# Attention values as 64-column weights, a transposed attention gate and probabilities scaled before their transpose, in a hybrid decoder layer

## What is computed

```python
u = rms_norm(h, norm_gain[layer])
z = jnp.einsum('bsd,de->bse', u, w_in[layer])
...
y_a = dsa_attention(q_a, k_a, v_a, q_i, k_i, w_i, topk).reshape(B, S, ATT_WIDTH)
y_a = y_a * jax.nn.silu(g_a)
...
y_r = retention(q_r, k_r, v_r).reshape(B, S, RET_V_WIDTH)
y_r = y_r * jax.nn.silu(g_r)
mix = jnp.concatenate([y_a, y_r], axis=-1)
h = h + jnp.einsum('bse,ed->bsd', mix, w_out[layer])
```

## Time and profile before

| | |
|---|---|
| median of 3 runs (lowest to highest) | 289.85 us (289.65 to 290.09) |
| the profiled execution, its own time | 289.56 us |
| its span in the profile | 287.8 us |
| PE busy | 280.0 us, 97% |
| DVE busy | 201.7 us, 70% |
| ACT busy | 143.1 us, 50% |
| POOL busy | 66.1 us, 23% |
| granted TensorE clock, mean | 0.994 |

### The profile page before, as it was taken

One profiled execution on the slowest core, in us unless ns is written; L12 is line 12 of the kernel. 1 busy time (PEld: TensorE's weight loads), 2 busy tenths in 40 slices (PEclk: granted clock), 3 DMA queues, 4 the chain that ended last, 5 costly groups with the idle time before them and its releaser, 6 DMA issues.

```text
span 287.8 us, 4402 instructions
## 1 busy us (share of the span) xinstructions
PE 280.0 (97%) x1506; PEld 239.7 (83%) x1506; DVE 201.7 (70%) x416; ACT 143.1 (50%) x305; POOL 66.1 (23%) x121
## 2 busy tenths in 40 slices
PE   8999999999999999999999999999999999999992
PEld 7998788888888788888888788888888888888891
DVE  3875879999999999999947545658734733763342
ACT  5887656526455224584357452583444563351230
POOL 1028822222200078766400102021020020000211
PEclk9999999999999999999999999999999999999997
DMA  7998404220422043052212220302200407311113
GB/s 268 410 365 336 147 3 146 73 68 8 146 74 75 20 146 110 18 146 75 75 48 98 75 73 0 122 26 74 76 0 2 146 0 260 107 36 36 75 78 142
DMA packets 13989, 30.10 MB, mean 105 GB/s; under 512 B 1168, under 2 KB 1680, under 8 KB 13968
## 3 DMA queue, kind: packets, MB, share of 16 engines
q1 hardware_dynamic: 13392, 29.04, 30.4%
q10 hardware_dynamic: 576, 0.79, 0.7%
HBM read 27.73 MB, written 2.10 MB: 104 GB/s over the span
## 4 chain that ended last, share of the span: by engine, by line
PE 65%; DVE 20%; issue 3%; POOL 1%; ACT 1%; POOLq 0%; DVEq 0%
PE bank L447 16%; PE bank L449 15%; PE bank L448 15%; PE bank L498 6%; DVE keys L1095 6%; DVE top L1093 5%; DVE w_lo L994 3%; PE bank L512 3%; DVE keys L1080 2%; PE bank L528 2%; PE bank L527 2%; DVE k_stack L1056 2%; PE bank L537 1%; PE bank L559 1%; PE bank L572 1%
## 5 line engine op out<-in xcount | busy, mean ns | idle before, releaser
L447 PE MATMUL bank<-w_hi,xT_hi 128*128 128x512 f32 (+1 forms) x296 | 116.5, 394 | 0.5 <-DVE w_lo L994 0.5
L449 PE MATMUL bank<-w_hi,xT_lo 128*128 128x512 f32 (+1 forms) x296 | 114.0, 385 | 0.0
L448 PE MATMUL bank<-w_lo,xT_hi 128*128 128x512 f32 (+1 forms) x296 | 113.8, 385 | 0.0
L447 PEld LDWEIGHTS bank<-w_hi,xT_hi 128*128 128x128 f32 x296 | 55.7, 188 | 11.6 <-DVE w_lo L994 1.2
L449 PEld LDWEIGHTS bank<-w_hi,xT_lo 128*128 128x128 f32 x296 | 55.6, 188 | 11.5
L448 PEld LDWEIGHTS bank<-w_lo,xT_hi 128*128 128x128 f32 x296 | 55.8, 188 | 9.8
L994 DVE TENSOR_TENSOR w_lo<-w_raw,w_hi 128x1024 fp32r<-128x1024 f32 x36 | 45.1, 1273 | 13.9 <-ACT w_hi L629 13.6
L629 ACT ACTIVATE w_hi<-w_raw 128x1024 fp32r<-128x1024 f32 x36 | 37.5, 1055 | 5.2 <-PE bank L449 3.4
L749 ACT ACTIVATE work<-work,small 128x128 f32<-128x128 f32 (+3 forms) x32 | 17.7, 555 | 31.8 <-DVE small L1118 31.7
L1093 DVE MAX8 top<-keys 128x8 f32<-128x256 f32 (+2 forms) x48 | 26.9, 560 | 1.3
L932 POOL TENSOR_TENSOR th<-zt,tab 128x64 f32<-128x64 f32 (+1 forms) x24 | 12.6, 523 | 60.0 <-ACT zt L678 56.4
(11 more groups left out here) (130 smaller groups left out, 370.9 us busy)
## 6 DMA issues: line engine op xcount, KB each, us to landing
w_raw<-in_w_in SPq DMA_DIRECT2D x28, 512.0 KB, 4.2
w_raw<-in_w_out SPq DMA_DIRECT2D x8, 512.0 KB, 3.7
retT<-in_x SPq DMA_DIRECT2D x8, 256.0 KB, 3.8
x_h<-in_first SPq DMA_DIRECT2D x2, 836.0 KB, 8.1
out<-x_h SPq DMA_DIRECT2D x4, 320.0 KB, 2.5
mix<-in_first SPq DMA_DIRECT2D x3, 418.0 KB, 5.2
v_ret<-in_x SPq DMA_DIRECT2D x2, 512.0 KB, 11.5
v_att<-in_x SPq DMA_DIRECT2D x2, 512.0 KB, 5.8
```

Source lines behind the costliest of these rows:

```text
L447: pe.matmul(o, xh, hi[:, kk, c0:c0 + w], start=first, stop=False)
L448: pe.matmul(o, xh, lo[:, kk, c0:c0 + w], start=False, stop=False)
L449: mm = pe.matmul(o, xl, hi[:, kk, c0:c0 + w], start=False, stop=last)
```

## The change

- `values(s)`: the weights are now the 64 columns of v of one head and the probabilities (128 columns) move; the two heads of a pair write PSUM partitions 0 to 63 and 64 to 127. So the attention output comes out transposed (`attT`) and only the retention half of `mix` is transposed (`transpose_mix`, four transposes instead of eight).
- The softmax divisor can no longer be applied to rows afterwards: `reciprocal(s)` (DVE) and `scale_probs(s)` (ACT) divide the probabilities before their transpose, which waits for `p_scaled` instead of `exp_done`.
- The attention gate's group is computed transposed (weights `w_hi`, moving `xT_hi` and `xT_lo`, again 24 matmuls of 512 columns). Its RMS factor then varies along the columns: POOL spreads it, PE transposes it (`turn_rstd`, slot 15), ACT writes `half_rstd_row`.
- The attention gate comes in slots 24 to 27 and the retention gate in 28 to 31. Outputs of blocks 0 and 1 wait in `qT` (`stash_y`).
- In a batch the scores come first. On ACT `probT_out` and `ret_squares` stand behind `exps`; on DVE `masked_max` stands ahead of the gates and of `decayed`, and `reciprocal` behind one top-k round. The rounds are 3 a slot up to slot 15 (before 17), 2 after.

```diff
@@ CHUNKS and constants
+          ("att_gate", 3 * ATT_W, ATT_W),
+          ("ret_gate", BASE + IDX_W + 2 * RH * RQK + RH * RV, RH * RV)]
...
-        n = min(4 if g <= 9 else 3 if g <= 17 else 2, ROUNDS * (MT - 1) - done)
+        n = min(4 if g <= 9 else 3 if g <= 15 else 2, ROUNDS * (MT - 1) - done)
@@ tensor
                     if g >= GROUPS:
-                        pe.wait_ge(mixlo_done, 2 * (m + 1))
+                        pe.wait_ge(att_lo_done, m + 1)
+                        pe.wait_ge(ret_lo_done, m + 1)
...
+                    if c == C_AG:
+                        e = slice(m * P, (m + 1) * P)
+                        pe.matmul(o, hi[:, kk, e], xT_hi[:, k, :], start=first, stop=False)
+                        pe.matmul(o, lo[:, kk, e], xT_hi[:, k, :], start=False, stop=False)
+                        mm = pe.matmul(o, hi[:, kk, e], xT_lo[:, k, :], start=False, stop=last)
+                        continue
...
             def values(s):
...
-                if p == 0 and b >= 1:
-                    pe.wait_ge(y_att_psum, b)
-                for hh in range(2):
-                    h = 2 * p + hh
-                    pe.wait_ge(pt_evac, 2 * s + hh + 1)
-                    for j in range(b + 1):
-                        mm = pe.matmul(att_ps[:, h * HD:(h + 1) * HD], probT[:, hh, j * P:(j + 1) * P],
-                                       v_att[:, j, h * HD:(h + 1) * HD], start=(j == 0), stop=(j == b))
+                if p == 0 and 1 <= b <= STASHED:
+                    pe.wait_ge(y_stashed, b)
+                elif p == 0 and b > STASHED:
+                    pe.wait_ge(att_mixed, b)
+                pe.wait_ge(pt_evac, 2 * s + 2)
+                for j in range(b + 1):
+                    for hh in range(2):
+                        h = 2 * p + hh
+                        mm = pe.matmul(att_ps[64 * hh:64 * hh + 64, p * P:(p + 1) * P], v_att[:, j, h * HD:(h + 1) * HD],
+                                       probT[:, hh, j * P:(j + 1) * P], start=(j == 0), stop=(j == b))
...
             def transpose_probs(s):
...
-                    pe.wait_ge(exp_done, 2 * s + hh + 1)
+                    pe.wait_ge(p_scaled, 2 * s + hh + 1)
...
-                        if s == steps_before_mix(m):
-                            pe.wait_ge(mixlo_done, 2 * m + hh + 1)
+                        if hh and s == steps_before_mix(m):
+                            pe.wait_ge(ret_lo_done, m + 1)
...
             def transpose_mix(m):
-                pe.wait_ge(att_mixed, m + 1)
                 pe.wait_ge(ret_mixed, m + 1)
                 pe.wait_ge(pt_evac, 2 * steps_before_mix(m))
...
+                if m >= 1:
+                    pe.wait_ge(ret_lo_done, m)
+                for j in range(KH):
+                    e = ATT_W + j * P
+                    mm = pe.transpose(trans_ps[1][:, j * P:(j + 1) * P], mix[:, m, e:e + P], ident)
+                mm.then_inc(mixT_mm, 1)
@@ scalar
+            def scale_probs(s):
+                b = s // PAIRS
+                act.wait_ge(rden_done, s + 1)
+                for hh in range(2):
+                    pr = prob[:, hh, 0:cols(b)]
+                    act.activation(pr, pr, ACT.Copy, scale=rden[:, s % 2, hh:hh + 1]).then_inc(p_scaled, 1)
+
+            def stash_y(b):
+
+                act.wait_ge(pv_done, PAIRS * (b + 1))
+                act.wait_ge(q_lo_done, b + 1)
+                act.activation(qT[:, :, b * P:(b + 1) * P], att_ps[:, :].rearrange("p (a t) -> p a t", a=PAIRS),
+                               ACT.Copy).then_inc(y_stashed, 1)
...
@@ vector
+            def reciprocal(s):
+
+                b, p = s // PAIRS, s % PAIRS
+                dve.wait_ge(exp_done, 2 * s + 2)
+                if s >= 2:
+                    dve.wait_ge(p_scaled, 2 * (s - 1))
+                dve.reciprocal(rden[:, s % 2, :], den[:, b % 2, 2 * p:2 * p + 2]).then_inc(rden_done, 1)
...
             def attention_out(b):
...
+                dve.tensor_tensor(attT[:, :, t], y, attT[:, :, t], ALU.mult).then_inc(att_mixed, 1)
@@ vector, the loop
+                if MT * C_AG <= g < MT * C_RG:
+                    att_z(g - MT * C_AG)
+                if 0 <= g - ATT0 < STEPS:
+                    masked_max(g - ATT0)
+                if MT * C_AG <= g < MT * C_RG:
+                    att_gate(g - MT * C_AG)
+                if MT * C_RG <= g < GROUPS:
+                    ret_gate(g - MT * C_RG)
                 if RET0 <= g < RET0 + 2 * MT and (g - RET0) % 2 == 0:
                     decayed((g - RET0) // 2)
-                if 0 <= g - ATT0 < STEPS:
-                    masked_max(g - ATT0)
                 if block_split_at(g) is not None:
                     block_q_lo(block_split_at(g))
+                for r in rounds_at(g)[:1]:
+                    topk_round(r)
+                if 0 <= g - ATT0 < STEPS:
+                    reciprocal(g - ATT0)
                 if RET0 <= g < RET0 + 2 * MT and (g - RET0) % 2 == 1:
                     retention_out((g - RET0) // 2)
...
-                for r in rounds_at(g):
+                for r in rounds_at(g)[1:]:
                     topk_round(r)
```

More of the change, by code:

```diff
@@ L57 @@
 STEPS = MT * PAIRS
-RET0 = MT * C_RG
+RET0 = MT * C_AG
+STASHED = 2
 TOPK0 = 6
@@ L213, in hymba_layer @@
         mix = sb("mix", [P, MT, 2 * ATT_W])
+        attT = mix[:, :, 0:ATT_W]
         first_in = [t[:, :, :].rearrange("p m c -> p (m c)") for t in (mix, x_h)]
@@ L594, in _ @@
                     transpose_group(g - 2)
+                if g == ATT0 - 1:
+                    turn_rstd()
                 if MT + 2 <= g <= 2 * MT:
@@ L771, in ret_squares, with att_hi, ret_hi, rstd_row @@
                                    accum_out=ret_ms[:, h:h + 1]).then_inc(ret_sq, 1)
[L773 removed]
+            def att_hi(m):
+                t = slice(m * P, (m + 1) * P)
                 act.wait_ge(proj_done, GROUPS - MT + m + 1)
[L775 to L778 removed]
+                act.wait_ge(att_mixed, m + 1)
+                act.activation(xT_hi[:, 0:KH, t], attT[:, :, t], ACT.Copy).then_inc(att_hi_done, 1)
+            def ret_hi(m):
+                act.wait_ge(proj_done, GROUPS - MT + m + 1)
+                act.wait_ge(mixT_mm, m + 1)
+                act.activation(xT_hi[:, KH:KT, m * P:(m + 1) * P], trans_ps[1][:, :].rearrange("p (k t) -> p k t", k=KH),
+                               ACT.Copy).then_inc(ret_hi_done, 1)
+            def rstd_row():
+                act.wait_ge(rstd_turned, 1)
+                act.activation(half_rstd_row[:, :], mid_ps[:, :], ACT.Copy).then_inc(rstd_row_done, 1)
             split_hi(QS)
@@ L816, in _ @@
                     block_q_rest(next_block)
+                if 0 <= g - ATT0 - 1 < STEPS:
+                    probT_out(g - ATT0 - 1)
                 if RET0 <= g < RET0 + 2 * MT and (g - RET0) % 2 == 1:
                     ret_squares((g - RET0) // 2)
+                if 0 <= g - ATT0 < STEPS:
+                    scale_probs(g - ATT0)
+                done = g - ATT0 - 2
+                if 0 <= done < PAIRS * STASHED and done % PAIRS == PAIRS - 1:
+                    stash_y(done // PAIRS)
+                if 0 <= g - (GROUPS - 2) < MT:
+                    att_hi(g - (GROUPS - 2))
                 if g >= GROUPS:
@@ L1129, in gate, with att_gate, ret_gate @@
+            def att_gate(n):
+                dve.wait_ge(tanh_done, n + 1)
+                dve.scalar_tensor_tensor(out=attT[:, n, :], in0=th[:, :], scalar=1.0, in1=attT[:, n, :], op0=ALU.add,
+                                         op1=ALU.mult).then_inc(agate_done, 1)
+            def ret_gate(m):
+                dve.wait_ge(tanh_done, MT + m + 1)
+                straight = m == MT - 1
+                half = mix[:, m, ATT_W:2 * ATT_W]
                 if not straight and tmp_last_read[0]:
@@ L1130, in gate @@
                     dve.wait_ge(*tmp_last_read[0])
-                dst = mix[:, m, w] if straight else tmp[:, :]
-                dve.scalar_tensor_tensor(out=dst, in0=th[:, :], scalar=1.0, in1=proj_ps[g % 2][:, :], op0=ALU.add,
-                                         op1=ALU.mult).then_inc(rgate_done if ret else agate_psum, 1)
+                dve.scalar_tensor_tensor(out=half if straight else tmp[:, :], in0=th[:, :], scalar=1.0,
+                                         in1=proj_ps[(MT * C_RG + m) % 2][:, :], op0=ALU.add,
+                                         op1=ALU.mult).then_inc(rgate_done, 1)
@@ L1248, in _ @@
                 if 0 <= g - (GROUPS - 1) < MT:
-                    mix_lo(g - (GROUPS - 1))
-                if MT * C_RG <= g < GROUPS:
-                    gate(g)
+                    ret_lo(g - (GROUPS - 1))
                 if g >= GROUPS:
```

164 lines of the change are left out of this document (84 added, 80 removed).

## The result

| | before | changed |
|---|---|---|
| median (lowest to highest), runs side by side | 289.97 us (289.51 to 290.32), 6 runs | 291.69 us (291.19 to 292.19), 6 runs |
| the profiled execution, its own time | 289.56 us | 291.19 us |
| its span | 287.8 us | 289.4 us |
| PE busy | 280.0 us | 275.5 us |

The ratio is 1.0061, 95% interval 1.0045 to 1.0078: slower by 0.6%, inside the range and on the forecast's side (292.3 us). A second set of runs gave 291.66 us (291.21 to 291.88), ratio 1.0068 (1.0051 to 1.0085), which is the base of the experiments.

The account below looks back on a forecast made before the run. PE was taken to bound the kernel, never waiting between 98.8 and 282 us. 289.56 - 4.35 of PE work + 6.75 of waits gave 292.0 us, 292.3 us by the median, range 287.5 to 295.2 us.

Parts of the forecast that it names:

- seven places named: PE waits in slots 17, 27, 28, 29, 30, 31 and 32, claimed to add up to 6.75 us.
- Slot 28's route: Lateness from slot 27 handed on to retention_out(1), for which ret_scores(2) waits: estimated 0.5 us (0 to 1).
- E + 4.07: Block 3: predicted end of the probT_out copies, E being the end of the batch's last attention transposes.
- E + 11.0: Slot 32: predicted end of ret_lo(1), counted from the last attention transposes' end; PE asks at E + 9.4.
- In the other slots I find slack: Claim of no new PE waits elsewhere, with slack from about 0 to 1.2 us or more.
- the term of slot 32: Head 1 of transpose_probs(15) waits for ret_lo(1), behind late retention_out(3) and split_lo: 1.6 us.
- PE's own work: PE work taken out: values 2.6 us, transpose_mix 1.75 us, the rest 0; sum -4.35 us.
- What would show it: Expected signs: values of block 3 at 1.2 us, four mix transposes, PE waits of about 1 us in six slots.
- Shorter chains: Rival: ACT and DVE chains shorter than laid out, slots 29 to 32 waiting 0.9 us, not 4.7; 288.5 us; chance 0.2.
- the 4.3 at which the sign would turn: PE waits together below 4.3 us would make the changed kernel faster.
- Pairs without edge cost: Rival: values runs its two-head pairs without edge cost, taking 8.8 us; 286.7 us in all; chance 0.1.
- The loop itself closes: Rival: ACT loses another 1.3 us, every slot from 28 on waits 0.5 to 1 us; 295.5 us; chance 0.15.

Follow-up runs that it names:

- the copies first: The changed kernel with probT_out moved back ahead of exps on ACT: 289.04 us, ratio 0.9974 to the kernel before.
- all orders: Changed kernel with probT_out ahead of exps, late loads ahead of the last weight unit, decayed and attention_out earlier on DVE, first reciprocal ahead of the top-k round: 286.86 us.
- the cut version: The kernel with all orders, values cut in two: key block 0 ahead of retention scores and transposes, the other blocks behind: 290.83 us.
- ACT's order: The kernel with all orders, plus retention squares ahead of the rest of the q block and stash_y ahead of the scaling on ACT: 286.32 us.

## Why the prediction was right, and where only the sum was

**The side and the mechanism were right.** PE never waited behind slot 16 before; the change took PE work out and put waits in, and the waits weighed more. The net loss was 1.7 us where 2.4 had been forecast. All seven places named are in the waits view, each with the releaser named. (Slot 28's route was only half right: the lateness was to be handed on from slot 27. With the copies first slot 27 has no wait and slot 28 still 0.63; without the scaling it is 0.33; with the squares ahead of the rest of the q block it is gone. So ACT's queue in slot 27 made it, 1.3 us of q-block splits among it.) With most of the waits taken out by order alone, the same operations run in 286.32 us, 3.4 us under the kernel before.

**The waits, term by term:**

| slot | 17 | 27 | 28 | 29 | 30 | 31 | 32 | 34 | sum |
|---|---|---|---|---|---|---|---|---|---|
| predicted, us | 0.9 | 0.65 | 0.5 | 0.8 | 1.0 | 1.3 | 1.6 | - | 6.75 |
| measured, us | 0.42 | 0.45 | 0.66 | 0.58 | 0.58 | 1.17 | 1.34 | 1.25 | 6.45 |

The seven places have 5.2 us in place of 6.75. In the chain to slot 32 E + 4.07 was E + 3.83, and E + 11.0 was E + 10.66: `exps` starts 0.1 us earlier than priced, and the two copies take 0.95 us by the starts, where 1.09, their busy time, had been taken. In slot 17 the two scalings of 128 columns took 0.6 us together, not 0.4 for each, and the top-k round ahead of `reciprocal(0)` was done by 107.8 us, not 108.1.

**The step that failed is the list of places.** "In the other slots I find slack" left out SP's queue. `split_lo` in slot 32 was known to be late (it is in the term of slot 32), but I followed from it only PE's wait, and not the DMA issue that waits for the same split. It is the prediction's own rule unapplied: name who waits for the late instruction, on each queue. It cost 1.3 us and nearly made up for what the other terms were too large by. So the sum of the waits (6.45 for 6.75) is right for two wrong reasons that cancel, and that is luck.

**PE's own work** was priced at -4.35 us and gave -4.85. `transpose_mix` is as priced: four transposes go in 0.35 to 0.38 us, and the insertion fell from 1.02 to 0.58 us between the matmuls around it, 0.44 in each of four slots. For `values` the gain was priced too low, -2.6 us where it gave -3.9. From the matmul ahead of the batch to the last one of the stretch of projection behind it, in slots without a wait, block 0 went up by 0.10 us (slots 18 to 21; +0.18 priced), block 1 down by 0.12 (22 to 25; -0.05 priced), block 2 down by 0.36 (26 and 29; -0.28 priced) and block 3 by 0.60 (31, and 30 with all orders; -0.50 priced), four steps each. The stretch behind has to be counted in: behind transposes the first projection matmul starts at once (0.03 us) and the next one 0.1 us late, so a count that ends at the first start makes a batch that ends in transposes look 0.1 us shorter than it is.

The term that was mis-sized is the edge of the old form, which had been priced at nothing. Slot 33 has `values` between 512-column matmuls on both sides, as `ret_kv` stands. With all orders, then in the kernel before:

```profile
244.34 0.39 PE L463 MATMUL bank<-w_hi,xT_lo 128*128 128x512 f32 x1
244.65 1.09 PE L525 MATMUL bank<-work,v_att 128*64 128x128 f32 x16
...
246.01 0.40 PE L462 MATMUL bank<-w_lo,xT_hi 128*128 128x512 f32 x1
```

```profile
246.03 0.40 PE L449 MATMUL bank<-w_hi,xT_lo 128*128 128x512 f32 x1
246.26 1.90 PE L498 MATMUL bank<-v_att,work 128*128 128x64 f32 x16
...
248.29 0.39 PE L448 MATMUL bank<-w_lo,xT_hi 128*128 128x512 f32 x1
```

By the prediction's own reckoning the new form takes 1.67 - 0.46 = 1.21 us, 0.33 over eight pairs of 0.11, and the old one 2.26 - 0.46 = 1.80, 0.07 over the 1.73 of the earlier trace rows. So the 0.35 us for the new form's edges was nearly right, and the same as the 0.32 to 0.35 of the second pair in the cut version; only what it replaced had edges too. Over sixteen steps 0.07 + 0.02 is 1.4 us, about the 1.3 between -2.6 and -3.9. (Start to the next instruction's start `values` takes 0.37, 0.59, 0.81 and 1.03 us, which leaves out what lies outside these two starts; the 1.2 us under "What would show it" had mixed the two.)

That makes 3.9 + 1.75 = 5.65 us taken out. The eight waits cost about 7.5 us by the starts around them, where the timeline gives 6.45, so 4.6 should be left; behind slot 16 it is 4.5, and the rest of the 4.85 lies before and around.

The Trainium skill's page TensorEngine Tiling (Array Packing) promises up to 2x in Theoretical Speedup. The trace has 1.73 against 1.03 us in block 3 and 0.39 against 0.37 in block 0, and the statement in its Key Properties that a change of mode drains the array is in keeping with the 0.32 to 0.35 us a pair, though no run tells a drain from another cost of the change. With the edges block 0 loses 0.10 us a step where the speedup alone would see a gain, as the prediction had it.

**The rivals.** *Shorter chains*: partly so, 5.2 us in the seven places, but over the 4.3 at which the sign would turn. *Pairs without edge cost*: excluded by the cut. *The loop itself closes*: not in the changed kernel. Slots 28 to 32 did wait one by one, but for the mix, the decayed scores, the copies and the splits; the only wait for the scaled probabilities is slot 17's, and most moves took their waits away for good. In two versions a part came back further on: 0.80 us in slot 31 with the copies first, 0.36 in slot 25 with ACT's order. Of what had been priced at nothing (the spread of the rounds, `turn_rstd`, the order of the gates), the wait of slot 16 is gone and none came between it and slot 17.

## What to carry to other kernels

Where one engine never waits, price a change by two lists, the work taken out and the waits put in; here the second was the longer, 6.45 against 4.85 us. When pricing the new form from a row with its edges, take the old form with its edges too. Then reorder before giving the change up: here the same operations run in 291.7 or 286.3 us by their order alone. For each instruction that gets late, list everybody who waits for it, the DMA queues included, since a load that needs nothing from it may be queued behind one that does. A chain of dependent small work (maximum, exponential, copy, scaling, transpose) wants its links in the order of its consumers on every engine, and its first input issued first.

## What the runs showed of the hardware

- Value products with 64-column weights for the two halves of the output partitions still overlap when they are issued one head after the other, by the starts over the first head's last four matmuls: block 1 took 0.60 against 0.59 us, block 3 1.51 against 1.03. One after the other, sixteen starts of 0.109 and the 0.15 over the pairs would be 1.9 (an estimate from these rows).
- One more pair of changes between 128-column and 64-column weights costs 0.32 to 0.35 us, without any work (3.97 us for 11, 0.4 of it waits). The pair around `values` in slot 33 costs 0.33, where the old form, with 128-column weights throughout, has 0.07.
- Two copies on ACT with a scale operand, SBUF to SBUF, take 1.23 us from the first start to the next instruction (512 columns, slot 31), two copies without one, out of PSUM, 0.95, and the two exponentials 1.43: the new operation lies between the two.
- PE's waits here cost more by the starts of its matmuls than the waits view says, about 7.5 against 6.45 us for all eight: slot 31's insertion took 1.94 us where slot 32's, without a wait, took 0.58, so 1.36 for a wait of 1.17.
